# Loads and sums between two layers of a diffusion step: what SyncE issues when, and where VectorE adds the first tile's rows

## The reference, cut to what matters

```
h    = rms_norm(x) * (1 + scale1) + shift1
proj = h @ w_in                 # u (pooling, 512) | query low rank 384 | key-value low rank 256 | rotary key 32
q    = rms_norm(rms_norm(cq) @ w_uq);  k, v = mla_keys(rms_norm(ckv), kr, w_ukv)
#      the latent tokens also read 128 cached context keys:  mla_keys(cache_ckv, cache_krope, w_ukv)
x    = x + gate1 * (concat(pool_mixer(u), attend(q, k, v)) @ w_out)
h2   = rms_norm(x) * (1 + scale2) + shift2
x    = x + gate2 * moe(h2)      # 16 experts of width 256, two for each token, weights w_gate, w_up, w_down
```

## Time and profile before

| what | value |
|---|---|
| median of three executions | 1051.77 us |
| the profiled execution: time, span | 1046.48 us, 1044.7 us |
| PE busy | 990.6 us, 95% |
| DVE, ACT, POOL busy | 602.6, 389.7, 203.7 us |
| the chain that ended last, by engine | PE 80%, DMA 9%, DVE 4%, issue 3%, POOL 2% |
| mean granted TensorE clock | 0.997 of full speed |
| last down products of layer one (L1253) begin | 514.88 us |
| second tile of layer two is turned (L820) | 541.13 us |

### The profile page before, as it was taken

One profiled execution on the slowest core, in us unless ns is written; L12 is line 12 of the kernel. 1 busy time (PEld: TensorE's weight loads), 2 busy tenths in 40 slices (PEclk: granted clock), 3 DMA queues, 4 the chain that ended last, 5 costly groups with the idle time before them and its releaser, 6 DMA issues.

```text
span 1044.7 us, 20986 instructions
## 1 busy us (share of the span) xinstructions
PE 990.6 (95%) x7528; PEld 546.8 (52%) x7529; DVE 602.6 (58%) x1352; ACT 389.7 (37%) x805; POOL 203.7 (19%) x309
## 2 busy tenths in 40 slices
PE   4999998999999989999989999999999998999997
PEld 1566555555544446555446665555554443555542
DVE  0334455656534787666574535576653568776657
ACT  1332224444311215666433322354431122666550
POOL 0123358000000100100142434910000011000003
PEclk9999999999999999999999999999999999999998
DMA  9960004578930589999981000348581167999948
GB/s 372 366 188 1 0 1 162 192 312 345 401 133 21 171 333 353 420 419 408 351 282 38 1 1 0 129 196 326 209 313 50 41 221 287 337 420 418 419 173 302
DMA packets 70742, 237.97 MB, mean 228 GB/s; under 512 B 11176, under 2 KB 26688, under 8 KB 56336
## 3 DMA queue, kind: packets, MB, share of 16 engines
q1 hardware_dynamic: 58720, 195.36, 48.8%
q0 software_dynamic: 6480, 23.60, 6.3%
q10 hardware_dynamic: 5472, 18.12, 4.3%
HBM read 211.54 MB, written 25.53 MB: 227 GB/s over the span
## 4 chain that ended last, share of the span: by engine, by line
PE 80%; DMA 9%; DVE 4%; issue 3%; POOL 2%; ACT 1%; ACTq 1%; SPq 1%; POOLq 0%; DVEq 0%
PE pair L1162 13%; PE bank L1244 12%; PE pair L855 8%; PE pair L870 7%; PE pair L1253 6%; PE pair L990 5%; PE pair L887 4%; PE bank L765 4%; PE bank L904 4%; PE bank L1026 4%; PE bank L1005 3%; PE pair L1208 2%; PE bank L839 2%; DMA big<-w_gate 2%; DMA big<-ada_w 2%
## 5 line engine op out<-in xcount | busy, mean ns | idle before, releaser
L1244 PE MATMUL bank<-big,actT 128*32 (+1 forms) x1520 | 179.6, 380 | 8.8 <-ACT actT L1616 5.3
L1616 ACT ACTIVATE actT<-big 128x1024 f32 x126 | 131.6, 1055 | 66.4 <-PE bank L1244 24.5
L1244 PE MATMUL bank<-actT 128*32 128x256 f32 x1680 | 150.6, 379 | 0.0
L1162 PE MATMUL pair<-big,actT 128*128 128x512 f32 x320 | 143.4, 599 | 0.0
L1244 PEld LDWEIGHTS bank<-big,actT 128*32 128x32 f32 x1520 | 96.7, 110 | 86.0 <-issue 24.4
L1253 PE MATMUL pair<-big 128*32 (+1 forms) x464 | 92.9, 596 | 1.8 <-ACT big L1627 1.5
L855 PE MATMUL pair<-big,actT 128*128 128x384 f32 (+1 forms) x320 | 93.7, 447 | 0.2 <-ACT actT L1367 0.2
L1162 PEld LDWEIGHTS pair<-big,actT 128*128 128x128 f32 x320 | 58.7, 190 | 65.8 <-issue 65.7
L1244 PEld LDWEIGHTS bank<-actT 128*32 128x32 f32 x1680 | 82.1, 110 | 0.1
L2184 DVE TENSOR_REDUCE mx<-pair 128x1 f32<-128x640 f32 x64 | 52.4, 819 | 46.1 <-PE pair L991 46.1
L1253 PE MATMUL pair<-actT,big 128*32 128x512 f32 x336 | 77.2, 595 | 0.5 <-issue 0.5
(11 more groups left out here) (338 smaller groups left out, 1608.2 us busy)
## 6 DMA issues: line engine op xcount, KB each, us to landing
big<-ada_w SPq DMA_DIRECT2D x48, 1024.0 KB, 7.8
big<-w_gate SPq DMA_DIRECT2D x32, 1024.0 KB, 9.4
big<-w_up SPq DMA_DIRECT2D x32, 1024.0 KB
big<-w_down SPq DMA_DIRECT2D x32, 1024.0 KB, 9.9
y_rows<-big ACTq DMA_DIRECT2D x24, 512.0 KB, 7.5
big<-w_out SPq DMA_DIRECT2D x4, 2048.0 KB, 14.3
big<-mod_rows SPq DMA_DIRECT2D x16, 512.0 KB, 7.6
h_rows<-big ACTq DMA_DIRECT2D x10, 512.0 KB, 3.0
```

The source lines that it names most:

```text
L1162: m = mm(dst, actT[:, k, t * P:(t + 1) * P], vw.wo[n][:, k, :], start=(k == order[0]), stop=(k == order[-1]))
L1244: m = mm(dst[lo:lo + m_, 0:DE], xgT[:, k, lo:lo + m_], weights(c, k % 4 * DE, DE), start=(k == 0), stop=(k == DC - 1), tile_position=(0, l ...
L1616: f(parts[1][i % 3], slot[:, i * PIECE:(i + 1) * PIECE], ACT.Copy).then_inc(w_a, 1)
```

## The change

```diff
@@ load_layer (SyncE)
                 sp.dma_start(vw.win_q[:, :, 0:QR], w_q[:, :, 0:QR]).then_inc(ld_win[0], 16)
-                sp.dma_start(vw.win_q[:, :, QR:], w_q[:, :, QR:]).then_inc(ld_win[1], 16)
+                if l == 0:
+                    sp.dma_start(vw.win_q[:, :, QR:], w_q[:, :, QR:]).then_inc(ld_win[1], 16)
...
                 if l > 0:
-                    used, b_st = by_layer[l - 1][9:11]
-                    n_more = sp.value_load(n_more_s[0:1, 0:1], min_val=NSTEP_MIN - 1, max_val=NSTEP - 1)
+                    used = by_layer[l - 1][9]
                     steps = sp.value_load(fin[0:1, 12:13], min_val=1, max_val=NSTEP)
-                    sp.wait_ge(b_st, n_more * 16)
                     sp.wait_ge(used, used_in(steps, 5))
+                    for w in range(2):
+                        sp.wait_ge(c_in[0][w], l * 16)
+                    sp.wait_ge(c_in[1][0], l * 32)
                 sp.dma_start(vw.wukv[:, :, :], ...).then_inc(ld_ukv, 16)
                 if l > 0:
-                    for w in range(2):
-                        sp.wait_ge(c_in[0][w], l * 16)
+                    sp.dma_start(vw.win_q[:, :, QR:], w_q[:, :, QR:]).then_inc(ld_win[1], 16)
                 sp.dma_start(vw.wuq[:, :, :], ...).then_inc(ld_uq, 16)
@@ VectorE, between the layers
                 else:
+                    add_last(l - 1, 0).then_inc(c_x, 1)
                     evac_low(0)
-                    link(add_early(l - 1, 0, 0))
-                    link(add_early(l - 1, 0, 1))
-                    add_last(l - 1, 0).then_inc(c_x, 1)
                     norm(0)
@@ VectorE, step
                     gate_rows(n)
-                    if last and l + 1 == DEPTH:
+                    if last:
                         link(add_early(l, 0, 0))
...
                             tt(yb[:, cols], pair[1][:, cols], yb[:, cols], ALU.mult).then_inc(e_y, 1)
-                        if l + 1 == DEPTH:
-                            link(add_early(l, 0, 1))
+                        link(add_early(l, 0, 1))
                         return
```

## The result

The kernel before took 1052.38 us in the median of twelve runs (1047.32 to 1058.36), the changed one 1059.24 us (1055.30 to 1064.16) on the same chip: a ratio of 1.0063, 95% interval 1.0040 to 1.0085, or 4 to 9 us slower. That is within 1% of no change, as forecast, and on its slow side. The forecast shift was +5.1 us; the medians differ by 6.9.

What follows compares the result with a forecast made beforehand. It took the wait for tile 0's and tile 1's rows between the layers, behind late gathers, as the bound. Tile 1's turn +3.3 us plus 1.8 for the clock gave +5.1 on 1051.77, so 1056.9 us, range 1049.4 to 1061.

Steps and rivals of the forecast that it cites:

- D: As a time origin: start of layer one's last down products, 514.88 us in the kernel before, 517.99 in the changed one.
- First, the store and the first gather: Between the layers: with SyncE's loads moved, the store lands in 3.9 us and the first gather starts 4.3 us earlier.
- rival B: Between the layers: store lands no faster, only the semaphore-to-gather gap is won; +7.2 us, 1059.0 us, chance 0.2.
- rival C: Between the layers: gathers start as before, the 2.95 us gap being POOL's own; +9.5 up to +13.9 us, chance 0.08.
- Second, VectorE's moved adds: On VectorE ahead of `yb`: `yb` 0.4 us late, costing nothing while `w_ukv` is later still, otherwise 0.5 us.
- Y: The yardstick: from D to the turning of layer two's second tile (tile 1), 26.25 us in the kernel before.
- Third, `w_ukv` behind four gathers: At kv_proj: fourth gather lands 9.5 us after the first starts, `w_ukv` 5.6 us later at 528.4; PE stands 4.9 us.
- Fourth, what follows: Behind the late kv_proj: tile 0 turned at 534.8, tile 1 9.6 us later at 544.4, +3.3 us.
- Fifth, the clock: On PE at kv_proj: half speed behind the 4.9 us pause, costing 1.8 us (bounds 0 and 3.4).
- Rival A: On PE at kv_proj: the clock holds through the pause; +3.3 us, 1055.1 us, chance 0.16.
- D's: The rival in which `w_ukv` lands by 523.2 and kv_proj runs as before; −2.4 us, 1049.4 us, chance 0.08.
- E's: The rival of cancelling ends: early store, quick `w_ukv`, clock held; +0.7 us, 1052.5 us, chance 0.06.

Runs made afterwards that it cites:

- pool_pad: Kernel before plus 24 semaphore increments in POOL's program ahead of its wait for the store; one run, 1046.09 us beside a median of 1054.39.
- store_alone: Changed kernel with the first query piece (1536 KB) also moved behind `w_ukv`; one run, 1059.67 us beside 1051.13.
- vector_only: Only VectorE's part of the change, with SyncE's order of the kernel before; ratio 1.0047 to the kernel before.
- sync_only: Only SyncE's part of the change, with VectorE's order of the kernel before; ratio 1.0070 to the kernel before.
- pad_awake: Changed kernel plus POOL's 24 semaphore increments and seven idle products, three ahead of early_rows and four ahead of kv_proj; ratio 1.0029 to the kernel before.
- after_pad: Changed kernel plus 24 semaphore increments in POOL's program ahead of its wait for the store; ratio 1.0051 to the kernel before.
- vector_awake: VectorE's part of the change alone, plus five idle products on PE ahead of layer one's early_rows; ratio 1.0045 to the kernel before.
- between: Kernel before with tile 0's add_last moved between its two early adds; ratio 0.9996.
- query_only: Kernel before with only the second query piece moved behind the four early gathers, `w_ukv` left in place; ratio 1.0017.
- best: Kernel before plus POOL's 24 increments, add_last between the two early adds, and one idle product instead of three ahead of tile 0's turn; ratio 0.9975.
- kv_behind: Kernel best with `w_ukv` behind tile 0's two gathers, kv_proj behind tile 0's turn replacing two idle products, four idle products where it stood; ratio 0.9972.

## Why the prediction was right, and where it wasn't

The forecast was +5.1 us and 1056.9 us, the measured median is 1059.24, inside the range. By the yardstick: tile 1 was to be turned at D + 31.3 and was at D + 32.5, 1.2 us later. The five steps, from the same D:

- **First, the store and the first gather: wrong by 3.8 us.** Forecast D − 1.6, measured D + 2.2. About half is the store, taken at 3.9 us, measured 5.5 and at D − 1.2 where D − 3.1 was forecast: rival B. The other half is the 2.6 us behind the semaphore, taken at 0.7: rival C. Each was named, and C's price, the first gather at 517.65 as before, is both together: it came nearest on this step, `w_ukv` landed at D + 17.9 by its sum and D + 17.0 as measured, and I had given it 0.08. I had read the gap in the earlier trace rows as `w_ukv`'s doing because `w_ukv` was what differed in the surroundings; pool_pad shows that POOL's own program does it.
- The rule of the Trainium skill that I had set beside B (DMA: Bandwidth & Descriptors, Queues, rings and completion order), that an engine goes round between its queue rows packet by packet, was right on the outcome: 5.5 us beside a backlog that was 1152 KB shorter, about 2.7 us in store_alone with it gone. The packets don't bear it out as the mechanism: for 3.6 us in the kernel before, and nearly 2 in the changed one, only SyncE's move, and only then do the two queues share.
- **Second, VectorE's moved adds cost nothing: wrong in the trace.** `yb` was to be 0.4 us late and was 4.3 (D + 8.1 against D + 3.8), as the sentence "every microsecond by which the gather is later delays it by one more" says once the first step fails. By itself it costs 4.8 us of Y (vector_only). In the whole change it is covered by the wait for `w_ukv`, which was my condition ("as long as w_ukv is later still"): PE was done with early_rows 1.5 us before `w_ukv` came.
- **Third, `w_ukv` behind four gathers: right, and the cause of the loss.** Landed at D + 17.0, forecast D + 13.5. First gather to issue took 9.7 us (forecast 9.5); the load took 4.9 (forecast 5.6). The fit of the Trainium skill (DMA: Bandwidth & Descriptors, Anatomy of one DMA), which that section gives for DMAs on GpSimd's path and not SyncE's, gave an estimate of 4.4 us. Issued at the same place the load took 4.9 to 5.1 us in four kernels (the changed one, store_alone, sync_only, pad_awake) and 5.8 in after_pad.
- **Fourth, what follows: right.** kv_proj to the next group 3.51 us (3.60), three idle products 2.57 (2.84), from tile 0's turn to tile 1's 9.49 (9.6).
- **Fifth, the clock: right in kind, wrong in place.** It fell behind a pause of 4.67 us, but of the one ahead of early_rows, and cost 2.9 us there, under cover of `w_ukv`. The 1.8 us in my sum did not occur. sync_only (5.15 us for kv_proj) and after_pad (6.64) show the cost that I had meant, 1.5 and 3.0 us.

So +3.4 for `w_ukv`'s landing, −1.8 for the clock and −0.5 for the smaller terms of the fourth step make the +1.2. The total came out near by luck: the first step was too early by 3.8 us, and a clock term of 1.8 us that never fell due, with the quicker load, made up for more than half of it. Rival A's sum would need a clock that held, D's a `w_ukv` in time, E's an early store, and none of these was seen. C's +9.5 at the least was too dear: the gathers did start 0.6 us earlier, the clock had recovered, and the load was quicker than in its sum.

**Still open.** In the changed kernel's profile 5.5 us more have gone by from tile 1's turn to the end than in the one before. Both profiled executions are off their medians (1061.39 beside 1059.24, 1046.48 beside 1052.38), so this need not hold for all. In layer two's last step ScalarE and VectorE wait for something that the trace has no name for:

```profile
1040.32 0.95 ACT L1668 ACTIVATE actT<-pair 128x128 f32<-128x128 f32 x5 [10.62 <-remote]
```

```profile
1040.24 1.29 DVE L2566 TENSOR_TENSOR big<-pair,big 128x512 f32<-128x512 f32 x2 [8.83 <-remote]
```

By the code both wait there for PE, whose records ahead of it end at 1033.5, almost 7 us earlier. PE then waits 7.83 us for ScalarE. Of the fourteen profiled executions seven have such a wait on ScalarE, of 5.7 to 10.6 us: the changed kernel, sync_only, vector_only, vector_awake, store_alone, between and pool_pad. The kernel before and query_only have none, nor any kernel with the pad but pool_pad. The medians follow Y without it (+6.3 of Y and +6.6 by the ratio for the change, +4.8 and +5.0 for vector_only), so I don't count it to the change. But the five kernels that have the pad and a ratio come out 0.7 to 2.7 us better by the ratio than by Y (sync_only, without it, 1.7 better, vector_awake 2.0 worse), and a part of best's and kv_behind's gain may lie there and not between the layers. No experiment here separates the two.

## What to carry to other kernels

When a load is moved behind a wait, price it by what stands behind its reader in that engine's order: here one late load of 1 MB held up everything behind kv_proj (Y 32.5 us), and with its reader moved as well, behind tile 0's turn, a late load cost little (kv_behind, 24.0). An operation put ahead of the one that feeds TensorE turns its own operand's delay into TensorE's, so such an add belongs behind that operation, as in the kernel before, however idle the engine is. A yardstick inside the kernel has to be read past its own end: in between the 1 us won at tile 1's turn was gone at tile 2's, by the clock. And a gap in a trace is not explained by the transfer that happens to lie beside it; lengthen the program ahead of it, or empty the queue, and see whether it moves.

## What the runs showed of the hardware

- A GpSimd program that goes on behind a long wait started its first indirect DMA 2.3 to 2.95 us after its last semaphore in layer one (eight kernels), with `w_ukv` in flight (2.3 to 2.95) or without it (2.4 to 2.6); with 24 semaphore increments put ahead of the wait it was 0.7 to 0.9 us (six kernels). A packet on instruction queue q14 lies in the long gap and in none of the short ones.
- ScalarE's store of 512 KB took 6.0, 5.5 and about 2.7 us with both, one and none of the query pieces issued ahead of it on SyncE's queue. Its first packet moved 3.6, some 2 and 0.8 us after the issue.
- A gather of 512 KB landed and was added within 4.8 us of its issue beside no load, and only after 7.1 us beside a load of 1 MB (kv_behind and best).
- Eight products that take 3.67 us at a granted clock of 1.00 took 6.54 at 0.50 behind a pause of 4.67 us, 6.20 behind one of 5.31, 5.37 behind 3.03, and 6.64 behind 3.16; behind 1.52 and 1.55 us they took 3.67. How long the clock stays at 0.50 is not told by the pause's length alone: 4.98 and 9.96 us were followed by 5.18 and 5.15. Eight products of 128x128 took 1.07 us behind pauses of 2.13 and 2.31, and 1.94 behind one of 2.45 (between).
- In these kernels a pause ahead of work that something else covers was free, and the same pause moved to work that nothing covers cost 3 us (after_pad), though every engine was earlier up to there.
